# A two-layer diffusion trunk on one core: the input loaded first, its modulation computed by pairs of pieces, and products of four projection items after each pair

## What is computed

```python
def _modulation(cond, w, b):
    m = jax.nn.silu(cond) @ w + b
    return [a[:, None, :] for a in jnp.split(m, N_MOD, axis=-1)]

def _modulate(x, shift, scale):
    return x * (1.0 + scale) + shift
...
    rq, rk, rv, rg, mq, mk, mv, mo, zg = _split(h @ w_in, EVEN_WIDTHS)
...
    log_gamma = jax.nn.log_sigmoid(ret_logit.astype(jnp.float32))
```

## Time and profile before

| | |
|---|---|
| median of 3 runs | 3058.77 us (3056.44 to 3060.44) |
| span of the profiled execution | 3056.9 us |
| TensorE busy | 2922.9 us, 96% of the span |
| VectorE, ScalarE, GpSimd busy | 1832.0, 1052.4, 92.2 us |
| mean granted TensorE clock | 0.978 |

### The profile page before, as it was taken

The page is one execution under the profiler, slowest core; times in us unless marked ns, Lnnn a source line. Parts: engine busy times, 40 slices in busy tenths (PEclk is TensorE's granted clock), DMA queues, the critical chain, the costliest instruction groups (busy, mean ns, idle before and its releaser), DMA issues. The chain is left out here.

```text
span 3056.9 us, 41091 instructions
## 1 busy us (share of the span) xinstructions
PE 2922.9 (96%) x16905; PEld 2602.5 (85%) x16905; DVE 1832.0 (60%) x3465; ACT 1052.4 (34%) x1590; POOL 92.2 (3%) x64
## 2 busy tenths in 40 slices
PE   8997899999999999999989879999999999999997
PEld 6985588999999999888869769999999999988886
DVE  4226577878544444466675568987854444446667
ACT  4332322445432322222233643344542323222222
POOL 1001200000000000000002002000000000000001
PEclk9998899999999999999999889999999999999999
DMA  8633475367744344266633123346774434426663
GB/s 276 202 117 143 149 256 199 152 251 290 286 151 156 135 155 169 76 234 210 230 138 110 64 85 135 114 152 241 291 282 155 165 131 159 166 79 225 211 237 131
DMA packets 208650, 543.11 MB, mean 178 GB/s; under 512 B 8016, under 2 KB 173264, under 8 KB 185680
## 3 DMA queue, kind: packets, MB, share of 16 engines
q1 hardware_dynamic: 207328, 539.67, 49.2%
q10 hardware_dynamic: 816, 0.74, 0.1%
q0 software_dynamic: 320, 0.07, 0.0%
HBM read 458.52 MB, written 81.92 MB: 177 GB/s over the span
## 5 line engine op out<-in xcount | busy, mean ns | idle before, releaser
L1061 PE MATMUL hidden_ps<-h_hi,u_hi 128*128 128x384 f32 x2048 | 694.2, 339 | 8.0 <-PEq L1072 6.4
L1061 PE MATMUL hidden_ps<-h_hi,u_lo 128*128 128x384 f32 x2048 | 686.3, 335 | 0.0
L1061 PE MATMUL hidden_ps<-h_lo,u_hi 128*128 128x384 f32 x2048 | 685.6, 335 | 0.0
L1700 PE MATMUL out_ps<-v_hi,act_hi 128*128 128x512 f32 x1488 | 584.6, 393 | 0.1
L1700 PE MATMUL out_ps<-v_hi,act_lo 128*128 128x512 f32 x1488 | 582.2, 391 | 0.0
L1700 PE MATMUL out_ps<-v_lo,act_hi 128*128 128x512 f32 x1488 | 581.6, 391 | 0.0
L1787 DVE TENSOR_TENSOR v_lo<-v_slot,v_hi 128x1024 fp32r<-128x1024 f32 x248 | 303.9, 1226 | 425.6 <-ACT v_hi L1738 425.6
L1738 ACT ACTIVATE v_hi<-v_slot 128x1024 fp32r<-128x1024 f32 x248 | 262.8, 1060 | 716.9 <-PE out_ps L1700 713.8
L1061 PEld LDWEIGHTS hidden_ps<-h_hi,u_hi 128*128 128x128 f32 x2048 | 385.0, 188 | 19.1 <-issue 14.9
L1061 PEld LDWEIGHTS hidden_ps<-h_lo,u_hi 128*128 128x128 f32 x2048 | 385.0, 188 | 4.2
L1061 PEld LDWEIGHTS hidden_ps<-h_hi,u_lo 128*128 128x128 f32 x2048 | 384.5, 188 | 0.0
(11 more groups left out here) (390 smaller groups left out, 3700.5 us busy)
## 6 DMA issues: line engine op xcount, KB each, us to landing
u_slot<-in_peer_u SPq DMA_DIRECT2D x64, 2048.0 KB, 7.9
v_slot<-in_peer_v SPq DMA_DIRECT2D x64, 2048.0 KB, 7.9
spread_gates<-spread SPq DMA_DIRECT2D x24, 2048.0 KB, 7.2
w_ring<-spread_gates SPq DMA_DIRECT2D x64, 768.0 KB, 9.9
hidden_early<-hidden_ring SPq DMA_DIRECT2D x36, 768.0 KB, 5.5
hidden_ring<-hidden_early SPq DMA_DIRECT2D x36, 768.0 KB, 11.4
ada_w_ring<-in_ada_w SPq DMA_DIRECT2D x48, 512.0 KB, 4.5
even_w_ring<-in_even_w SPq DMA_DIRECT2D x16, 1024.0 KB, 4.8
```

Source lines behind the costliest of these rows:

```text
L1061: mm = pe.matmul(PH_[:, b, 0:T], u[:, b, k * P:(k + 1) * P], x[:, k, :], start=(k == 0 and part == 0), stop=(k == KB - 1 and part == 2))
L1700: mm = pe.matmul(PO[:, t, c, :], a[:, t * P:(t + 1) * P], x[:, c * CH:(c + 1) * CH], start=(o == 0 and part == 0), stop=(o == N_KEYS - 1 a ...
```

## The change

X is loaded first. The pieces are taken in the order 0, 4, 1, 5, 2, 6, 3, 7, so that each pair holds shift and scale of two blocks. The two chunks of `W` are loaded ahead of the first and second pair. All transposes of X come ahead of the first piece, and so do the transposed norm gains (`ln_turned`, `lnc_done`). After each pair the bias is added for its two blocks, they are scaled and split, and TensorE does for these two blocks the 24 matmuls of all four items of chunks 0 and 1, whose four sums stay open in `PJ` until the fourth pair. The turns n = 0 and 1 of the loop then have no items. `high_part(1)` and `low_part(1)` stand behind the first pair's blocks. The dummy multiplications become 6 ahead of the pairs and 4 in each pair.

```diff
@@ sync
-                    for m in range(FIRST):
-                        if m == RING:
-                            for t in range(TT):
-                                sp.dma_start(X[:, t, :], I["x"][t]).then_inc(x_in, 16)
-                        if m >= RING:
-                            sp.wait_ge(first_used, m - RING + 1)
-                        sp.dma_start(A0[:, m % RING], ada_half(0, m)).then_inc(first_in[m % RING], 16)
-                    for n in range(SLOTS):
-                        sp.dma_start(W[:, n], I["even_w"][n]).then_inc(w_in[n], 16)
+                    for t in range(TT):
+                        sp.dma_start(X[:, t, :], I["x"][t]).then_inc(x_in, 16)
+                    for i, m in enumerate(PAIRED):
+                        if i % 2 == 0 and i // 2 < SLOTS:
+                            sp.dma_start(W[:, i // 2], I["even_w"][i // 2]).then_inc(w_in[i // 2], 16)
+                        if i >= RING:
+                            sp.wait_ge(first_used, i - RING + 1)
+                        sp.dma_start(A0[:, i % RING], ada_half(0, m)).then_inc(first_in[i % RING], 16)
@@ tensor
+                    def first_mod(i):
+                        pe.wait_ge(first_in[i % RING], 16 * (i // RING + 1))
+                        if i >= 2:
+                            pe.wait_ge(first_row, i - 1)
+                        mod_half(pe, PR, A0[:, i % RING], i, first_used)
...
+                    def first_products(g):
+                        for item in range(PER * SLOTS):
+                            n, i = divmod(item, PER)
+                            if g == 0 and i == 0:
+                                pe.wait_ge(w_hi, n + 1)
+                                pe.wait_ge(w_lo, n + 1)
+                            for k in (2 * g, 2 * g + 1):
+                                if item == 0:
+                                    pe.wait_ge(h_split, k + 1)
+                                for part, (w, h) in enumerate(((WH, HH), (WH, HL), (WL, HH))):
+                                    mm = pe.matmul(PJ[:, item, 0:T], w[:, n, k, i * P:(i + 1) * P], h[:, k, :],
+                                                   start=(k == 0 and part == 0), stop=(k == KB - 1 and part == 2))
+                            if g == PAIRS - 1:
+                                mm.then_inc(item_done, 1)
...
+                    pe.wait_ge(pick_made, 1)
+                    pe.wait_ge(x_in, 16 * TT)
+                    for kb in range(KB):
+                        turn_x(kb)
                     pe.wait_ge(ln_in, 32)
...
+                    pe.wait_ge(lnc_done, 1)
+                    keep_warm(6)
+                    pe.wait_ge(xt_taken, KB)
+                    for g in range(PAIRS):
+                        first_mod(2 * g)
+                        first_mod(2 * g + 1)
+                        first_columns(2 * g)
+                        first_columns(2 * g + 1)
+                        keep_warm(4)
+                        first_products(g)
                     for n in range(NCH):
...
-                        for i in range(items(n + 1) - items(n)):
+                        for i in range(items(n + 1) - items(n) if n >= SLOTS else 0):
@@ scalar
                     high_part(0)
-                    act.wait_ge(mod_made, 1)
-                    for kb in range(KB):
...
-                    high_part(1)
+                    for g in range(PAIRS):
+                        for i in (2 * g, 2 * g + 1):
+                            act.wait_ge(first_used, i + 1)
+                            if i >= 2:
+                                act.wait_ge(first_turned, i - 1)
+                            act.activation(ROW[:, i % 2, :], PR[:, i % 2, 0:HALF_COLS], ACT.Copy).then_inc(first_row, 1)
+                        act.wait_ge(mod_made, g + 1)
+                        for kb in (2 * g, 2 * g + 1):
...
+                        if g == 0:
+                            high_part(1)
                     act.dma_start(LG[:, 0, :], spread(I["ret_logit"], 2 * H)).then_inc(logit_in, 16)
                     act.wait_ge(logit_in, 16)
                     act.wait_ge(cst_in, 16)
@@ vector
+                    low_part(0)
...
+                    for g in range(PAIRS):
+                        ks = slice(2 * g, 2 * g + 2)
+                        dve.wait_ge(first_turned, 2 * g + 2)
+                        v.seq(dve.tensor_tensor(mods[:, :, ks, :], sums[:, :, ks, :], bias[:, :, ks].unsqueeze(3).broadcast_to([P, 2, 2, 2]), ALU.add))
+                        m = MOD[:, 0, KB + 2 * g:KB + 2 * g + 2, :]
+                        dve.tensor_scalar_add(m, m, 1.0).then_inc(mod_made, 1)
+                        for kb in (2 * g, 2 * g + 1):
+                            dve.wait_ge(ht_made, kb + 1)
+                            v.seq(dve.tensor_copy(HH[:, kb, :], HT[:, kb, :]))
+                            dve.tensor_tensor(HL[:, kb, :], HT[:, kb, :], HH[:, kb, :].bitcast(F32), ALU.subtract).then_inc(h_split, 1)
+                        if g == 0:
+                            low_part(1)
```

More of the change, by code:

```diff
@@ L144, in mod_half @@
             mm.then_inc(used, 1)
[L146 to L151, removed]
         def cond_slot(k, q):
@@ L219, in even_project @@
                 assert REST == NCH and GATE_AT + 4 < NCH
+                PAIRED = [a + g for g in range(FIRST // 2) for a in (0, FIRST // 2)]
+                PAIRS = len(PAIRED) // 2
+                assert PER * SLOTS == 4 and KB == 2 * PAIRS
                 aw_in = [sem(st, f"ada_w_in{n}") for n in range(2)]
@@ new lines, in first_columns @@
+                    def first_columns(i):
+                        pe.wait_ge(first_row, i + 1)
+                        for c in range(2):
+                            at = (PAIRED[i] * 2 + c) * 2
+                            mm = pe.matmul(PM[:, at:at + 2], ROW[:, i % 2, c * P:(c + 1) * P], PICK[:, 0:2], start=True, stop=True)
+                        mm.then_inc(first_turned, 1)
+                    def first_products(g):
[12 more added lines that the diff above has]
+                                mm.then_inc(item_done, 1)
@@ L322, in _, with keep_warm @@
+                    def keep_warm(n):
+                        for _ in range(n):
+                            pe.matmul(PG[:, 0:P], ident, ident, start=True, stop=True)
+                    pe.wait_ge(pick_made, 1)
+                    pe.wait_ge(x_in, 16 * TT)
+                    for kb in range(KB):
+                        turn_x(kb)
                     pe.wait_ge(ln_in, 32)
@@ L328, in _ @@
                         hi, lo = WH[:, n % PARTS], WL[:, n % PARTS]
[L329 removed]
+                        for i in range(items(n + 1) - items(n) if n >= SLOTS else 0):
                             item = items(n) + i
[L331 to L332 removed]
+                            pe.wait_ge(item_taken, item - 3)
                             for k in range(KB):
[L334 to L335 removed]
                                 for part, (w, h) in enumerate(((hi, HH), (hi, HL), (lo, HH))):
@@ L359, in _ @@
                         if n == 0:
-                            pe.wait_ge(lnc_done, 1)
                             pe.wait_ge(gate_in, 8 * 16)
@@ L550, in _ @@
                         dve.tensor_copy(HT[:, kb, :], PJ[:, kb % 4, 0:T]).then_inc(xt_taken, 1)
-                    dve.wait_ge(bias_in, 16)
-                    dve.wait_ge(first_turned, FIRST)
-                    mod_add(dve, v, 0, PM, 0, 2)
-                    dve.sem_inc(mod_made, 1)
-                    low_part(0)
-                    for kb in range(KB):
-                        dve.wait_ge(ht_made, kb + 1)
-                        v.seq(dve.tensor_copy(HH[:, kb, :], HT[:, kb, :]))
-                        dve.tensor_tensor(HL[:, kb, :], HT[:, kb, :], HH[:, kb, :].bitcast(F32), ALU.subtract).then_inc(h_split, 1)
-                    low_part(1)
                     dve.wait_ge(ln_turned, 1)
                     dve.tensor_copy(LNC[:, :, :, :].rearrange("p a n k -> p (a n k)"), PG[:, 0:2 * DEPTH * 2 * KB]).then_inc(lnc_done, 1)
+                    low_part(0)
+                    dve.wait_ge(bias_in, 16)
+                    parts = lambda x: x.rearrange("p (a k) j -> p a k j", a=2)
+                    mods, sums = parts(MOD[:, 0, 0:2 * KB, :]), parts(PM[:, 0:4 * KB].rearrange("p (c j) -> p c j", j=2))
+                    bias = B[:, 0:2 * KB].rearrange("p (a k) -> p a k", a=2)
+                    for g in range(PAIRS):
[10 more added lines that the diff above has]
+                            low_part(1)
                     dve.wait_ge(a_step, 3)
```

15 lines of the change are left out of this document (5 added, 10 removed).

## The result

Slower: 3068.75 us (median of 6 runs, 3064.62 to 3072.77) against 3058.94 (6 runs), a ratio of 1.0032 with a 95% interval of 1.0022 to 1.0042. That is 9.8 us by the medians; 12 were predicted, in a range of 3062 to 3082 us.

The account below looks back on a forecast made before the run. The prediction took TensorE as the bound, with the start of chunk 2's products setting the time. A 10.4 us later start plus 1.6 us of low clock, added to the 3058.8 median, gave 3071 us, range 3062 to 3082.

Parts of the forecast that it names:

- Bound and measure: TensorE is continuously busy from chunk 2 on, so the start of chunk 2's products, 68.16 before, moves all that follows.
- Loads: X lands at 9.6, the pairs at 18.7, 27.8, 33.9 and 40.0; from the second pair on, not the bound.
- Ahead of the pairs: TensorE's transposes, gains and dummies before the first pair run from 9.6 to 19.4, covered by loads but for 0.7 us.
- One pair: From both pieces there to the last product, the serial bias, scaling, split and products take 10.4 us a pair.
- The first pair: Bias made at 24.0, last products 8.2 us later; second pair starts at 32.2, the fourth at 53.0.
- ScalarE's chain: Logits issued at 56.6, then 2.0 + 10.84 + 4.77 + 4.29 + 0.1: chunk 2 at 78.6, 10.4 us later than before.
- The gates: ScalarE is not at the gates before 70, so late gate weights cost nothing, and without this cover at most 1 us.
- The clock: After TensorE's idle 8 us before chunk 2, half clock for 3.3 us costs 1.6 us, added once.
- the rival's low clock: Rival: the clock is low through all pairs, each costing 5.8 us more; 3089 us, chance 0.12.
- Sum: 10.4 us for chunk 2's later start plus 1.6 for the clock is 12.0, added to the median of 3058.8.
- The pairs did not keep up with the loads: Rival claimed they do: fourth pair starts at 40.0, chunk 2 at 65.6; 3056 us, chance 0.09.
- Swallowed later: Rival: a later part of this stage has slack and absorbs the delay; 3059 us, chance 0.09.

Follow-up runs that it names:

- e11: Kernel before with only the load order changed: X first, two chunks of W ahead of the first and third piece; ratio 1.0013 against the kernel before.
- e10: Changed kernel with the pairs doing chunk 0 only and chunk 1's products back in their own turn; ratio 1.0019 against the kernel before.
- e4: Changed kernel with only TensorE's order changed, the next pair's pieces multiplied ahead of this pair's products; ratio 1.0030 against the kernel before.
- e6: Changed kernel with 28 dummy multiplications on TensorE behind the turn of chunk 1; ratio 1.0025 against the kernel before.
- e7: Changed kernel with high_part(2) ahead of the gates on ScalarE and the decay tables behind pairs 3 and 4; ratio 1.0013 against the kernel before.
- e12: e8 with the first pair's items 0 and 1 ahead of the second pair's pieces; 3053.54 us against 3058.42 for the kernel before, ratio 0.9984.
- e9: Kernel before with only high_part(2) moved ahead of the gates on ScalarE; ratio 0.9996 against the kernel before.
- e8: e7 with e4's order on TensorE; ratio 0.9994 against the kernel before.

## Why the prediction was right

*Bound and measure.* Right: the time follows the start of chunk 2; 8.65 of the 9.8 us stand at the turn behind it.

*Loads.* The order alone costs the kernel before 4.2 us (e11); in the changed kernel the pairs hide it, as written: no pair after the first waits for a piece. The loads were earlier than counted: X was there at 8.11 instead of 9.6, and the wait for the first pair's second piece ended at 16.64, not at 18.7.

*Ahead of the pairs.* Mis-sized, and the one large error of the sum. I started the first pair at 19.4; its first piece was used at 15.27 and its second at 16.64. The transposes took 4.57 instead of 5.6 us, as the clock was at full rate before they ended, and the dummies 1.61 instead of 3.0.

*One pair.* Right: 10.2 us against 10.4. (Its sum has two slips of 0.1 us that cancel: 0.90 + 0.95 + 0.1 is 1.95, not 2.05, and the 3.9 is added as 3.8.)

*The first pair.* The bias was made at 19.27, not 24.0; from there to the second pair's start at 27.73 it is 8.5 us against 8.2. So the fourth pair starts at 48.17 instead of 53.0, and this is nearly all of the difference in the sum.

*ScalarE's chain.* Each term held: 2.55 us for the logits (2.0 taken), 10.83, 4.76, 4.29. The 2.55 rests on the moment of issue: in e10 and e4, 3.9 and 5.7 us earlier, the same load took 5.2 and 8.2.

*The gates.* This is the step that failed, though it cost the sum nothing. I wrote that ScalarE "is not at the gates before 70, so that costs nothing, and without this cover at most 1 us". Measured, tables and gates ended within 0.01 us of each other. My own sum had them at 56.6 + 2.0 + 10.8 = 69.4 and 63.4 + 1.0 + 5.4 = 69.8, and I did not see what it means: the delay has two causes of equal length, and taking away the tables gains 0.6 us, not 8. What they have in common is the thing to name. Before, the 48 products of chunk 1 lay behind the gates and covered ScalarE's gate functions and both parts of chunk 2. The change moved these products ahead of the gates, and the 9 us from the gates' end to chunk 2 lie open.

*The clock.* Right in kind, too small: 2.6 us (e6) instead of 1.6. I took the length of the fall from the earlier trace rows, 3.3 us; here it lasted until about 80, 5.7 us into the products. The Trainium skill ("TensorE: Matmul & The Clock Gate", "HAM oscillation — how this bites in real kernels") says that idle gaps bring the low clock back; the stretch from 70 with 0.50 agrees. In the pairs, with holes of about 1.5 us, the rival's low clock came only once in this trace: the granted clock was 0.50 from 22 to 25, and the later pairs ran at full rate. e7 had more of it.

*Sum.* 6.0 for the start of chunk 2 and 2.65 for the clock, against 10.4 and 1.6. So 8.65 us are shown where 12.0 were summed. The medians say 9.8; the other 1.1 us lie behind the turn of chunk 2, and no run shows what they are. The forecast was right in its direction and its path; that the number came within 2 us is in part luck, as the start was 4.4 us too late, the clock 1 us too small, and the rest was not in the sum. The upper bound of + 23 also left out the 1.6 us of the sum's own clock term.

*The rivals.* The pairs did not keep up with the loads. In e4 they nearly do, by TensorE's order: the fourth starts at 40.25, where the rival had 40.0. But its chunk 2 starts at 74.13, not at 65.6, because the logits take 8.2 us among the large loads and not 2.0. At chunk 2's turn it gains nothing, and the 2 us by the medians lie within the intervals. "Swallowed later" is false for the medians: + 9.8 for + 8.65.

## What to carry to other kernels

When work is moved forward out of an engine's queue, ask what it covered where it stood: here 8 us of another engine's preparation. When two chains end together, removing one shows next to nothing; price both, and test both at once. And cutting a phase into rounds pays its latency in every round unless the next round's independent work is put into the gap: 10.2 us a pair in the changed kernel, 7.1 in e4 and e12. And a small load issued earlier need not land earlier: 5.7 us gained at its issue were gone at its landing in e4.

## What the runs showed of the hardware

**The clock falls elsewhere, too, and not in every execution alike.** First and last start of two tiles' matmuls, in the trace of the kernel before and then of the changed one: the first products of the stage that follows, and the first transposes behind the mLSTM stage:

```profile
L632 PE MATMUL att_ps<-qk_t x24: 275/275/422, 213.2 to 226.1; 128*128 128x128 f32 x24
...
L822 PE MATMUL mix_t_ps<-CST,mix x24: 272/273/477, 279.8 to 314.2; 128*128 128x128 f32 x24
```

```profile
L657 PE MATMUL att_ps<-qk_t x24: 274/276/349, 221.8 to 233.6; 128*128 128x128 f32 x24
...
L847 PE MATMUL mix_t_ps<-CST,mix x24: 272/273/473, 285.8 to 320.2; 128*128 128x128 f32 x24
```

The delay is 8.6 us at the first and 6.0 at the second. Between 200 and 240 us the granted clock is 0.91 and 0.95 before and 1.00 after. From the first of these moments to the second it takes 66.6 us before and 64.0 after, and in the other kernels of this study between 63.4 and 69.7. e9, which is within 0.2 us of the kernel before at chunk 2's turn, takes 63.4. So an execution can win or lose some 3 us there, whatever the first stage did; this is why single spans and medians differ here.

The clock also falls inside the stage, with TensorE busy throughout. Busy time by stretch between the turns behind chunk 4 and chunk 5, after 16 thin matmuls of 6 columns (1.9 us), in e8 and, for the same work, in the kernel before:

```profile
96.00:98.00 2.00, 2.00 (x8) 2.00 (x7) 1.52 (x2) 0.00 (x0) 0.36 (x1) 0.50 0.17 52
```

```profile
101.70:103.70 2.00, 2.00 (x13) 2.00 (x13) 1.49 (x2) 0.00 (x0) 0.39 (x1) 1.00 0.15 43
```

From the one turn to the other it takes 12.3 us in the traces of the kernel before, the changed kernel, e4, e6, e10 and e12, and 13.9 in those of the other seven, e8 and e9 among them. Of the 5.7 us that e8 is ahead at chunk 2's turn 4.1 are left at chunk 5's, and 1.4 at the first transposes behind the mLSTM stage (278.4). Whether that holds for its other runs, and so explains its 0.8 by the median, is not tested; they go from 3053.62 to 3059.88.

**Transposes did not keep the clock low.** The 24 transposes of X are all that TensorE does from 8.11 to 12.6 in the changed kernel. The duration in ns (least, median, most) of all 24, of those from 12 us on, and of the same 24 in the kernel before:

```profile
L291 PE MATMUL proj_ps<-CST,X x24: 272/421/448, 8.1 to 12.4; 128*128 128x128 f32 x24
```

```profile
L291 PE MATMUL proj_ps<-CST,X x7: 272/273/273, 11.8 to 12.4; 128*128 128x128 f32 x7
```

```profile
L296 PE MATMUL proj_ps<-CST,X x24: 272/273/307, 23.5 to 27.6; 128*128 128x128 f32 x24
```

The first took 421 ns, the last ones 273, the duration that they have at full rate in the kernel before. (The granted clock reads 1.00 all the while from the start of the span, so here it is the durations that tell.) The Trainium skill ("TensorE: Matmul & The Clock Gate", "Part 4: PE-mode transpose") says that the full rate does not engage for transposes, as they do not count as TensorE's activity in the same way. Here the measurement differs, if these are transposes in its sense: each shows as one row where a multiplication by the same identity shows as two, but the rows don't name the mode. The kernel before began with the thin matmuls of the pieces, and their 16 rows took 1.89 us until 18 us and 1.04 from 24.91 on.
